# A fused block of retention, latent attention, convolution and feed-forward: rotary scores of a head in one product of 64 rows, gate strips shifted by two heads, products of ones at seven places, ada columns at other places

## The reference

```python
c_q = rms_norm(z[..., :o1], q_norm_g)
k_rope = rope(z[..., o2:o3][:, :, None, :], pos)[:, :, 0, :]
q = (c_q @ w_uq).reshape(B, S, MLA_HEADS, MLA_NOPE + MLA_ROPE)   # 16 heads, 128 + 64
q_nope, q_rope = q[..., :MLA_NOPE], rope(q[..., MLA_NOPE:], pos)
s = (q_nope . k_nope + q_rope . k_rope) * 192 ** -0.5            # causal, then softmax
return (jax.nn.silu(gate) * o) @ w_out
# rope(x): x1, x2 = halves of 32; [x1 * cos - x2 * sin, x2 * cos + x1 * sin]
```

## Time and profile before

| | us |
|---|---|
| median of 3 runs | 936.27 |
| the three runs | 930.68, 936.27, 941.46 |
| the profiled execution | 934.69 |
| its span, first to last instruction | 932.9 |
| mean granted clock of TensorE | 0.964 |

### The profile page before, as it was taken

One profiled execution on the slowest core, in us unless ns is written; L12 is line 12 of the kernel. 1 busy time (PEld: TensorE's weight loads), 2 busy tenths in 40 slices (PEclk: granted clock), 3 DMA queues, 4 the chain that ended last, 5 costly groups with the idle time before them and its releaser, 6 DMA issues.

```text
span 932.9 us, 15862 instructions
## 1 busy us (share of the span) xinstructions
PE 875.4 (94%) x5650; PEld 795.5 (85%) x5650; DVE 676.7 (73%) x947; ACT 494.7 (53%) x719; POOL 52.5 (6%) x61
## 2 busy tenths in 40 slices
PE   7999999999989999999899989999787599999996
PEld 5899999888868999999778879999685599999884
DVE  7868668656766676776656775799768778888565
ACT  5354554545545554656335555445632588888441
POOL 0800000000011000000000010070000000000000
PEclk9999999999999999999879998999999699999998
DMA  7657566477625747374537544435234255556551
GB/s 264 228 185 266 177 225 215 167 255 282 217 103 187 246 134 254 100 246 152 181 113 290 205 137 143 171 116 180 90 110 170 82 183 184 183 185 230 182 181 45
DMA packets 48279, 169.43 MB, mean 182 GB/s; under 512 B 5489, under 2 KB 6001, under 8 KB 48242
## 3 DMA queue, kind: packets, MB, share of 16 engines
q1 hardware_dynamic: 40608, 142.70, 44.7%
q10 hardware_dynamic: 7634, 26.25, 8.0%
HBM read 167.88 MB, written 1.05 MB: 181 GB/s over the span
## 4 chain that ended last, share of the span: by engine, by line
PE 78%; DVE 13%; DMA 3%; issue 3%; ACT 2%; ACTq 0%; POOL 0%; DVEq 0%; SPq 0%
PE bank L391 14%; PE bank L392 14%; PE bank L393 14%; PE bank L425 7%; PE bank L427 7%; PE bank L426 7%; DVE wlo L1258 3%; DMA ada_raw<-ada_in 2%; PE bank L753 1%; DVE ada_acc L1274 1%; PE bank L566 1%; PE bank L567 1%; PE bank L568 1%; PE bank L495 1%; PE bank L676 1%
## 5 line engine op out<-in xcount | busy, mean ns | idle before, releaser
L1258 DVE TENSOR_TENSOR wlo<-raw,whi 128x1024 fp32r<-128x1024 f32 (+1 forms) x265 | 318.5, 1212 | 137.7 <-ACT whi L806 135.3
L806 ACT ACTIVATE whi<-raw 128x1024 fp32r<-128x1024 f32 (+1 forms) x265 | 273.9, 1041 | 270.6 <-PE bank L393 138.7
L391 PE MATMUL bank<-H,whi 128*128 128x256 f32 x976 | 285.1, 292 | 8.0 <-DVE wlo L1258 2.4
L392 PE MATMUL bank<-H,whi 128*128 128x256 f32 x976 | 278.6, 285 | 0.0
L393 PE MATMUL bank<-H,wlo 128*128 128x256 f32 x976 | 278.6, 285 | 0.0
L391 PEld LDWEIGHTS bank<-H,whi 128*128 128x128 f32 x976 | 189.7, 194 | 10.1 <-DVE wlo L1258 4.8
L392 PEld LDWEIGHTS bank<-H,whi 128*128 128x128 f32 x976 | 189.9, 195 | 0.6
L393 PEld LDWEIGHTS bank<-H,wlo 128*128 128x128 f32 x976 | 189.7, 194 | 0.0
L425 PE MATMUL bank<-whi,Y 128*128 128x512 f32 x216 | 86.3, 400 | 0.0
L426 PE MATMUL bank<-wlo,Y 128*128 128x512 f32 x216 | 86.0, 398 | 0.0
L427 PE MATMUL bank<-whi,Y 128*128 128x512 f32 x216 | 85.9, 398 | 0.0
(11 more groups left out here) (240 smaller groups left out, 1249.3 us busy)
## 6 DMA issues: line engine op xcount, KB each, us to landing
raw<-w_head SPq DMA_DIRECT2D x48, 512.0 KB, 4.4
ada_raw<-ada_in ACTq DMA_DIRECT2D x48, 512.0 KB, 4.3
raw<-w_up SPq DMA_DIRECT2D x44, 512.0 KB, 3.3
raw<-w_down SPq DMA_DIRECT2D x22, 512.0 KB, 4.2
raw<-w_uq SPq DMA_DIRECT2D x24, 384.0 KB, 3.0
raw<-w_ret_out SPq DMA_DIRECT2D x16, 512.0 KB, 4.8
raw<-w_ple_gate SPq DMA_DIRECT2D x16, 512.0 KB, 4.2
raw<-w_mla_gate SPq DMA_DIRECT2D x16, 512.0 KB, 4.4
```

The lines of the kernel that those rows point to most:

```text
L391: mm(o, whi[:, s, c], a[:, 0, :], start=start, stop=False)
L392: mm(o, whi[:, s, c], a[:, 1, :], start=False, stop=False)
L806: activation(whi[:, s, 0:n], raw[:, s, 0:n], ACT.Copy).then_inc(hi_done, 1)
L1258: tt(wlo[:, s, 0:n], raw[:, s, 0:n], f32(whi[:, s, 0:n]), ALU.subtract).then_inc(lo_done, 1)
```

## The change

- Rotary features: a strip now holds two heads of 64 rows each, with the halves side by side. The rotated query is x times cos plus swapped x times sin (the sign is in the angle table). The swapped x comes from a new product with a permutation (swap, 128x512, fp32), between strips 4 and 5 of every group, from a copy XQ that ACT makes. For the key, both orders come from the weights. scores has one product of 64 rows for each head and query block, in place of two of 32.
- Gate strips: two before the groups (were four), four in groups 0 to 2, for later heads, and two in the last group (had none), which thereby has the same order as the others as far as it goes. gate_evac_one evacuates single strips.
- hold(b, n): n products of ones by ones, 128x128 in fp32, whose result nobody reads, at seven places.
- mod_columns(0, 2) stands before the wait for o_free; mod_columns(3, 2) in the last group between values(1) and turn(2), into another bank.
- One more constant (swap) is loaded from ACT's queue at the start.

The diff, cut to its core; the block counts at the top, the loads and the argument lists follow from it:

```diff
+            def hold(b, n):
...
+                for _ in range(n):
+                    mm(b[:, 0:P], ones[:], ones[:], start=True, stop=True)
...
             last.then_inc(row_spread, 1)
+            hold(PB[1], 10)
...
             turn_tile(U_PRE0, 1, WT, PB[3])
+            hold(PB[1], 8)
...
                 strip(B_HEAD + 11, halves(b)[1], H, 12, i)
+            mod_columns(0, 2, GD[1])
             pe.wait_ge(o_free, RET_HEADS + 1)
-            mod_columns(0, 2, GD[1])
...
             turn_tile(U_QKV, 1, WT, PB[3])
-            for j in range(4):
-                if j % 2 == 0:
-                    b = free_a(A_MG + j // 2)
-                strip(B_MG + j, halves(b)[j % 2], H)
+            for j in range(2):
+                strip(B_MG + j, halves(free_a(A_MG + j))[0], H)
...
-                    if gates:
+                    if gates == 4:
...
                         strip(base + 8 + j, halves(GA[j // 2])[j % 2], H, 12, i)
+                    elif j < gates:
+                        pe.wait_ge(act_free, at(A_GRP + 5 + j, 6))
+                        strip(base + 8 + j, halves(GA[j])[0], H, 12, i)
...
                             mm(GD[h % 2][:, c], QN[:, h, q0:q0 + P], KN[:, h, 0:n], start=True, stop=False)
-                        for d in range(2):
-                            for h in (h0, h0 + 1):
-                                r = slice(32 * h, 32 * h + 32)
-                                last = mm(GD[h % 2][:, c], QR[r, d, q0:q0 + P], KR[r, d, 0:n], start=False, stop=d == 1)
-                                if d == 1 and q0 == P:
-                                    last.then_inc(s_psum, 1)
+                        for h in (h0, h0 + 1):
+                            r = slice(64 * (h % 2), 64 * (h % 2) + 64)
+                            last = mm(GD[h % 2][:, c], QR[r, h // 2, q0:q0 + P], KR[r, 0:n], start=False, stop=True)
+                            if q0 == P:
+                                last.then_inc(s_psum, 1)
...
                 latent_strip(4, GA[0][:, 0:T])
+                pe.wait_ge(xq_ready, at(1, 1))
+                mm(M3[:, 0:2 * T], swap[:], XQ.rearrange("p a t -> p (a t)"), start=True, stop=True).then_inc(swapped, 1)
...
                 values(1)
+                if o == 3:
+                    mod_columns(3, 2, GA[1][:, T:2 * T])
...
             with pe.Fori(0, 3) as i:
-                group(0, i, True)
-            group(3, 0, False)
+                group(0, i, 4)
+            group(3, 0, 2)
             pe.wait_ge(mo_gated, 4 * 4 + 1)
-            mod_columns(3, 2, GD[1])
...
             mod_columns(5, 1, M0)
+            hold(M1, 8)
...
                               for n in range(8)])
+            pe.wait_ge(act_free, A_UP + 2)
+            hold(GA[0], 14)
...
             token_pass(B_WO, 1, 1, H, 0, 4)
+            hold(GA[0], 20)
             turn_tile(U_LNB, 0, WT, PB[2])
+            hold(GA[0], 34)
             turn_tile(U_LNB, 1, WT, PB[3])
+            hold(GA[0], 8)
...
             act.dma_start(cnt[:], cnt_in).then_inc(in_const, 16)
+            act.dma_start(swap[:], swap_in).then_inc(in_const, 16)
...
             act.wait_ge(trig_ready, 2)
-            for j in range(4):
-                split(B_MG + j)
-                if j == 2:
-                    evac(B_MG + 1, 0, pair(G, 0), ACT.Silu)
-            evac(B_MG + 3, 1, pair(G, 1), ACT.Silu)
+            def gate_evac_one(base, f, g, per=0, i=0):
...
+                used(base, per, i)
+                activation(dyn(G, g, 1), GA[f][:, 0:T].unsqueeze(1), ACT.Silu).then_inc(act_free, 1)
...
+            split(B_MG)
+            split(B_MG + 1)
+            gate_evac_one(B_MG, 0, 0)
+            gate_evac_one(B_MG + 1, 1, 1)
...
                         activation(V[:, 1, :], M1, ACT.Copy).then_inc(mv_ready, 1)
+                    if j == 3:
+                        used(base + 3, 12, i)
+                        activation(XQ, wide(M2), ACT.Copy).then_inc(xq_ready, 1)
...
                     if j == 11:
-                        evac(base + 9, 0, dyn(G, 4 * i + 4 * o + 4, 2), ACT.Silu, 12, i)
+                        evac(base + 9, 0, dyn(G, 4 * i + 4 * o + 2, 2), ACT.Silu, 12, i)
...
                         turned(3)
-                if gates:
-                    evac(base + 11, 1, dyn(G, 4 * i + 4 * o + 6, 2), ACT.Silu, 12, i)
+                if gates == 4:
+                    evac(base + 11, 1, dyn(G, 4 * i + 4 * o + 4, 2), ACT.Silu, 12, i)
                 else:
-                    evac(base + 7, 1, pair(QN, 1), ACT.Copy, 12, i)
-                    for h in range(4):
-                        exps(h)
-                        if h % 2 == 1:
-                            turned(h - 1)
-                            turned(h)
+                    exps(2)
+                    exps(3)
+                    turned(2)
+                    turned(3)
+                    for j in range(2):
+                        gate_evac_one(base + 8 + j, j, 4 * o + 2 + j)
...
             with act.Fori(0, 3) as i:
-                group(0, i, True)
-            group(3, 0, False)
+                group(0, i, 4)
+            group(3, 0, 2)
...
             dve.wait_ge(trig_ready, 2)
-            rope(GD[0], TC[:, 0, :].rearrange("p (a t) -> p a t", a=2), TC[:, 1, :].rearrange("p (a t) -> p a t", a=2),
-                 2, KR, 2 * RET_HEADS + 1, dve_free, V_KR + 4, qr_ready, 2, frees=2)
-            for j in range(4):
+            tt(TC[:, 0, 0:T], GD[0][:, 0:T], TAB[:, 2, :], ALU.mult).then_inc(rope_tmp, 1)
+            tt(TC[:, 1, 0:T], GD[0][:, T:2 * T], TAB[:, 3, :], ALU.mult).then_inc(dve_free, 2)
+            dve.wait_ge(rope_tmp, 2 * RET_HEADS + 1)
+            dve.wait_ge(dve_free, V_KR + 4)
+            tt(KR, TC[:, 0, 0:T], TC[:, 1, 0:T], ALU.add).then_inc(qr_ready, 2)
+            dve.wait_ge(qr_ready, 2)
+            for j in range(2):
...
                         used(base + 3, 12, i)
-                        rope(M2, TC[:, 0, :].rearrange("p (a t) -> p a t", a=2),
-                             TC[:, 1, :].rearrange("p (a t) -> p a t", a=2), 2, QR, 2 * RET_HEADS + 2 + o, rope_read, 1 + o,
-                             qr_ready, 4 + 2 * o, (1, 1, 2), i)
+                        ta, tb = (TC[:, n, :].rearrange("p (a t) -> p a t", a=2) for n in range(2))
+                        tt(ta, wide(M2), over(TAB[:, 2, :], 2), ALU.mult).then_inc(rope_tmp, 1)
+                        dve.wait_ge(swapped, at(1, 1))
+                        tt(tb, wide(M3), over(TAB[:, 3, :], 2), ALU.mult).then_inc(rope_read, 1)
+                        dve.wait_ge(rope_tmp, at(2 * RET_HEADS + 2, 1))
+                        dve.wait_ge(rope_read, at(1, 1))
+                        tt(QR, ta, tb, ALU.add).then_inc(qr_ready, 2)
+                        dve.wait_ge(qr_ready, at(4, 2))
...
                         ada(27 + 4 * o, 1, 1, 4, i, o)
-                        if gates:
-                            masked(0)
-                            masked(1)
+                        masked(0)
+                        masked(1)
...
                         gate_head(1)
-                if not gates:
-                    for h in (0, 2):
-                        masked(h)
-                        masked(h + 1)
-                        if h == 2:
-                            gate_head(0)
-                            gate_head(1)
-                        normed(h)
-                        normed(h + 1)
+                if gates == 2:
+                    gate_head(0)
+                    gate_head(1)
+                    normed(2)
+                    normed(3)
+                dve.wait_ge(act_free, at(A_GRP + 2 + (5 if gates == 4 else 6), 6))
...
             with dve.Fori(0, 3) as i:
-                group(0, i, True)
-            group(3, 0, False)
-            mod_read(2, 3, 2, GD[1])
+                group(0, i, 4)
+            group(3, 0, 2)
+            mod_read(2, 3, 2, GA[1][:, T:2 * T])
...
     kr = mi[:, 1024:1088]
-    kr = cat([kr[:, 0:32]] * 4 + [kr[:, 32:64]] * 4, axis=1)
+    kr = cat([kr, kr, kr[:, 32:64], kr[:, 0:32], kr[:, 32:64], kr[:, 0:32]], axis=1)
...
         hs = uq[:, 4 * g:4 * g + 4]
-        uqs += [_strips(hs[:, :, 128:160].reshape(768, 128)), _strips(hs[:, :, 160:192].reshape(768, 128)),
+        uqs += [_strips(hs[:, 0:2, 128:192].reshape(768, 128)), _strips(hs[:, 2:4, 128:192].reshape(768, 128)),
...
     inv_m = np.tile((10000.0 ** (-np.arange(half_m, dtype=np.float64) / half_m)).astype(f), 4)
+    inv_m = inv_m * np.tile(np.repeat(np.array([-1, 1], f), half_m), 2)
...
         "x_in": x[0].reshape(2, P, D).transpose(1, 0, 2), "p_in": np.stack([_features(p[0, 0]), _features(p[1, 0])]), "pos_in": positions[0],
-        "cols_in": cols, "rows_in": rows, "mask_in": mask, "tri_in": tri, "cnt_in": cnt, "ident_in": np.eye(P, dtype=f), "ada_in": ada,
+        "cols_in": cols, "rows_in": rows, "mask_in": mask, "tri_in": tri, "cnt_in": cnt, "ident_in": np.eye(P, dtype=f),
```

(1 more changed line is left out.)

31 lines of the change are left out of this document (17 added, 14 removed).

## The result

The changed kernel takes 920.79 us (median of 4 runs, 914.9 to 924.81), the kernel before 936.77 beside it (4 runs): ratio 0.9854, 95% interval 0.9812 to 0.9896. The prediction was 921.0, in a range of 912 to 931. The profiled execution took 922.1 us, its span is 920.3 and its mean granted clock 0.985 (before: 934.69, 932.9, 0.964).

A forecast was written before the change was run, and what follows sets the result against it. TensorE (PE) was taken as the bound, with 78% of what ended last. Terms summing to -15.35 us took the profiled 934.69 to 919.3; with 1.6 for the median, 921.0, range 912 to 931.

The forecast's parts named there:

- Start: Kernel start: one more DMA and 10 products of ones delay the transposes, +1.6; possibly another slow stretch, +0.8.
- Columns and clock: End of retention: columns fill the wait for o_free, -1.8; half the slow stretch behind goes, -1.3.
- Scores: Attention groups 0 to 2: a call saves 0.85 us by halved products, swap costs +0.95 a group; -1.65 in all.
- the first rival: Scores: 64-row products of two heads run one after the other, so only the swap's cost remains; 926.4 us, chance 0.08.
- Gate strips and group 3: 5.76 us of strips leave before group 0, and group 3 reaches out_product 2.0 us earlier despite holding them; -7.7.
- I leave that as it is: Out_product after group 3: its first products run slow now and were taken to stay so; no gain counted.
- Layer norm A: Eight products of ones delay transposes by 0.7, then the earlier clock saves 2.0 on mod_row; -1.0 taken.
- Pool: Before the pointwise products: 14 products of ones fit the 4.5 us wait and the slow stretch goes; -1.7.
- Layer norm B: Products of ones in three waits: transposes -0.95, strips behind at full clock -2.5; taken as -2.6.
- -0.9 as a rival: Layer norm B: the clock falls once more inside it, term -0.9 instead of -2.6; 922.7 us, chance 0.15.
- The last group bound by its own chain: Group 3: masks, exponentials, norms, turns and gates wait for one another; term -3.7, 925 us, chance 0.15.
- Slow products of ones: Rival for all places: products of ones cost 0.43 us each at the slow clock throughout; 940.8 us, chance 0.09.

The follow-up runs named there:

- e3: Changed kernel with both mod_columns calls back at their old places; 923.61 us, ratio 0.9925 to the kernel before.
- e5: The changed kernel itself, unaltered, timed and profiled again on another chip; 915.98 us, ratio 0.9829 to the kernel before.
- e11: e6 with the last group's 16 one-column products split, eight after values(1), eight after values(3); 911.54 us, ratio 0.9756 to the kernel before.
- e6: e2 with longer later products of ones (22 for 14, 27 for 20, 41 for 34); 913.28 us, ratio 0.9800 to the kernel before.
- e8: Changed kernel with 32-row rotary products, no swap product or swap load, no products of ones at the start; 913.63 us, ratio 0.9808.
- e12: e11 with 11 more products of ones in two waits of the stage near 268 us; 910.85 us, ratio 0.9764 to the kernel before.
- e1: Changed kernel without any of its products of ones; 921.34 us, ratio 0.9876 to the kernel before.
- e2: Changed kernel without the 18 products of ones at the start; 914.48 us, ratio 0.9814 to the kernel before.

## Why the prediction was right, and where it was not

The number was right within 0.3 us; the steps were less so, and a hit as close as that is luck. The four runs lie between 914.9 and 924.8, the profiled one is 2.8 us above its forecast of 919.3, and the sum in the profile is -12.6, not -15.35: 4.8 were lost in a stretch that no term had and the 1.7 of the pool did not come, while layer norm A gave 1.8 more than forecast, the start 1.3, group 3 1.2 and the stage behind it 1.0. The medians differ by 16.0.

**Start: +2.4 predicted, +1.1.** The first strip starts at 16.8, within the 15.5 to 17 forecast, though 1.2 us of the delay is a longer wait for the row constants (3.5 in place of 2.3) and not the edit. The second head is only 1.1 late: the clock first rises at 12.6, not 19.4, and the extra slow stretch of +0.8 did not come; the one at 46.7 went instead. Between two profiles of one kernel the second head moves by 0.9 us, with either kernel.

**Columns and clock: right.** -3.1 predicted, -3.6. The columns gave 2.7 and not 1.8, since they ran at full clock and took 3.5 us, not 4.3; the stretch behind them gave 1.0 (1.3 predicted). e3 confirms the move as the largest difference.

**Scores: the mechanism right, the size off.** The two heads do run side by side, which rules out the first rival. A call saves 0.64 us and not 0.85 (3.30 to 2.66): a pair of half the products takes 0.42 and 0.64, not 0.32 and 0.53. The step that failed is the halving. In the trace, products of one height start 0.11 us apart (128 columns) or 0.21 (256), but about 0.1 us more passes at each change between full height and 32 or 64 rows, and at each change back. So the 0.64 and 1.06 of the 32 rows held four steps and 0.2 us of changes, and only the steps were halved. With 0.86 for the swap a group saves 0.4. The chain of ada loads and masks took part of that: PE waits 0.64 at the second scores of group 2, where it waited 0.37. But the chain is no fixed 16.4 us from strip 4 to the turn of head 1: in group 1 it took 15.8, in group 2 16.9, and in e5 15.8 and 16.0. And group 0 does wait for a DMA: DVE idles 2.3 us for ada data there.

**Gate strips and group 3: -7.7 predicted, -8.5 in the profile.** From the end of strip 4 to out_product the prediction had 29.6, and it took 28.6. In e5, the same kernel, it took 30.9, so that there the term is -6.2; the seven profiles named under e11 average 38.9 us for group 3 against 40.9 in the two of the kernel before, which with the 5.4 before the groups makes -7.4. But it is the sum of strips and columns; the strips alone time at -2, so the part of the text that gives the strips 5.76 by themselves is borne out by profiles (5.4) and not by the timing.

**Out_product: "I leave that as it is" was wrong by 2.3 us.** In the kernel before a half-speed stretch ran from 476.8 to 483.6, into out_product; now it ended at 470.0, before it. The stage behind it gave 1.3 back in waits for DVE.

**Layer norm A: -1.0 predicted, -2.8.** The clock did not fall, so the eight products of ones took 2.0 us and not 2.7 and did not delay the transposes: the +0.7 of the sum did not come. The transposes gave 0.8 and mod_row 1.8.

**Pool: -1.7 predicted, 0.** The prediction took a wait filled by two thirds for a wait that is gone. 2.0 us stayed idle and the stretch came back at 668.0 in this execution.

**Layer norm B: right**, -2.6 against -2.7, 0.5 of it up to the first strip and 2.2 behind it. The clock did not fall between its tiles in the first profile. By the Trainium skill, "TensorE: Matmul & The Clock Gate", Part 4, transposes do not count as activity for the clock; on that ground the prediction had -0.9 as a rival. In the changed kernel the clock stayed up (1.00 from 719.2 to 739.6); in e5 a stretch of 3.4 us does begin at 705.0, in the first tile's transposes. Neither tests the rule, since products of ones stand on both sides. The start does: in four of the nine profiles without products of ones there (e6, e8, e11, e12) the clock rose at 11.2 to 12.5 us, during or just behind 16 transposes, when PE had run nothing else since its four one-row products ended at 6.0 to 7.3 us. In e6 the rise at 11.24 falls inside them, and they take 3.53 us, not 3.65. There the traces disagree with the rule.

**How much of it is the clock.** With "lost clock" for (1 - mean granted clock) x span, the runs of the kernel before beside e5 lose 32.2 us on average and those of the changed kernel 11.3, 20.9 less. Among the runs of the kernel before alone, the span grows by 0.6 to 0.7 us for each us lost (fits over 17 runs on either of two chips). It is tempting to price the 20.9 at that rate, which gives 13 to 15 of the 15.7 us between the mean spans, but e1 and e2 show that it does not hold for the products of ones: between them the lost clock falls by 16.1 us and the span by 6.1, 0.38 for each. These raise the clock where PE has little other work; in e1 PE is busy for 8.5 us of the 20.5 at half speed in layer norm B. An estimate from these numbers is 6.1 us for the later products of ones and, at 0.6 to 0.7, about 3 for the other 4.8 us of lost clock: 9 of the 15.7. The prediction gave the clock 5.8 by name (retention 1.3, layer norms 3.6, pool 1.7, less 0.8 at the start) and, unnamed inside group 3, about 4.9, half of the 9.86 us of PE work at half speed in the earlier trace rows. The two kinds can't be parted fully, since a wait filled is also a clock held.

**Rivals.** The last group bound by its own chain is true in part: 0.76 us of wait and the half-speed turns remained, and e11 took them up. Slow products of ones were seen only at the start in the first profile (0.44 against 0.23), and in e5 behind the first tile of layer norm B, where the 34 took 9.14 us and not 7.76 and filled their wait without making the second tile later. That is also the one time the clock fell inside layer norm B in this kernel.

## What to carry to other kernels

Where PE waits for another engine for some us, or runs a row of one-column products, look at the granted clock behind it: by the estimate above that decided over half of the gain here. Move such products into a wait and split them between waits. Filler products of full width helped in long waits in the middle of the kernel (6.0 us, e1 against e2) and brought nothing measurable at the start. Do not price them by the mean granted clock: part of the clock that they hold is clock that no other work would have used. Before a difference between two single profiles is given to an edit, profile each kernel twice: here group 3 of the same kernel took 38.0 and 40.3 us, and a stretch of 3 to 10 us came and went.

## What the runs showed of the hardware that was not expected

- Products of 64 rows for two heads start together, as those of 32 rows do. Each change between full height and either of them, and each change back, costs about 0.1 us: at full height or at 32 or 64 rows the starts are 0.11 us apart (128 columns), across a change 0.21. Halving the number of products leaves this part as it is.
- 16 one-column sums (32 passes) take 3.63 us at full clock, 0.11 a pass, and 5.87 where the clock falls within them (e3). All 26 runs of 16 in the 14 profiles have a fall of the clock 1.3 to 4.7 us after their start. Behind the four runs of eight in the last group of e11 and e12 there is none.
- At the start no fall or rise is recorded in the first 11 to 20 us (10.7 to 19.7 in the 14 profiles), and the window of 5 to 14.4 us in e2 is printed as 1.00, while 16 transposes take 3.65 us in it, as at half clock.
- The clock rose inside a run of 16 transposes, at 11.24 us in e6 and at 11.70 in e11. Before these PE had run only four one-row products, and had then been idle for 1.7 to 1.9 us.
